# Slabs of the modulation weights as the stationary operand, three output tiles started together, one more buffer for split weights

## What is computed

```python
def ada_modulation(cvec, w, b):
    m = jax.nn.silu(cvec) @ w + b          # w: 1024 x 3072 per layer, cvec: c and c_ctx
    return jnp.split(m, 3, axis=-1)
hx = modulate(rmsnorm(x, norm_w[l]), shift_x[:, None], scale_x[:, None])   # h*(1+scale)+shift
px = split_proj(hx @ w_in[l])
...
mod = (c_act @ ada_w[i] + ada_b[i])[:, None, :]                            # second block, 6 x 1024 each
h = rmsnorm_2(x, norm_g[i, 0]) * (1.0 + sc_m) + sh_m
```

## Time and profile before

| | us |
|---|---|
| median of 3 runs (range) | 2013.99 (2012.77 to 2014.24) |
| profiled execution | 2014.52 |
| its span | 2012.7 |
| PE busy / PEld busy | 1940.7 / 1670.6 |
| DVE busy / ACT busy | 1420.9 / 903.8 |
| mean DMA rate | 149 GB/s |

### The profile page before, as it was taken

One profiled execution on the slowest core, in us unless ns is written; L12 is line 12 of the kernel. 1 busy time (PEld: TensorE's weight loads), 2 busy tenths in 40 slices (PEclk: granted clock), 3 DMA queues, 4 the chain that ended last, 5 costly groups with the idle time before them and its releaser, 6 DMA issues. The chain is left out here.

```text
span 2012.7 us, 31617 instructions
## 1 busy us (share of the span) xinstructions
PE 1940.7 (96%) x12194; PEld 1670.6 (83%) x12194; DVE 1420.9 (71%) x2648; ACT 903.8 (45%) x1657; POOL 0.2 (0%) x4
## 2 busy tenths in 40 slices
PE   7999999999999999999989999999999999999997
PEld 2788887767888887898878999687799979989997
DVE  1549956568889993677667997563688558968864
ACT  2422324545323332434456544464565546456553
POOL 0000000000000000000000000000000000000000
PEclk9999999999999999899999999999999999999999
DMA  8323321114666662543224986556555525135542
GB/s 271 124 87 101 90 78 42 42 32 157 199 205 202 201 199 84 163 152 105 84 74 137 290 281 225 174 162 199 193 184 184 165 92 168 64 105 189 184 163 95
DMA packets 293252, 299.21 MB, mean 149 GB/s; under 512 B 4960, under 2 KB 292704, under 8 KB 292976
## 3 DMA queue, kind: packets, MB, share of 16 engines
q1 hardware_dynamic: 293104, 297.19, 46.1%
HBM read 296.12 MB, written 1.05 MB: 148 GB/s over the span
## 5 line engine op out<-in xcount | busy, mean ns | idle before, releaser
L485 PE MATMUL bank<-h_hi,w_hi 128*128 128x256 f32 (+1 forms) x2912 | 929.8, 319 | 26.3 <-ACT h_hi L1094 7.2
L486 PE MATMUL bank<-h_lo,w_hi 128*128 128x256 f32 (+1 forms) x2912 | 915.1, 314 | 0.0
L487 PE MATMUL bank<-h_hi,w_lo 128*128 128x256 f32 (+1 forms) x2912 | 914.9, 314 | 0.0
L1525 DVE TENSOR_TENSOR w_lo<-ring,w_hi 128x1024 fp32r<-128x1024 f32 (+2 forms) x444 | 502.1, 1135 | 296.1 <-ACT w_hi L1008 282.2
L485 PEld LDWEIGHTS bank<-h_hi,w_hi 128*128 128x128 f32 x2912 | 557.4, 191 | 79.8 <-issue 14.6
L487 PEld LDWEIGHTS bank<-h_hi,w_lo 128*128 128x128 f32 x2912 | 557.7, 192 | 32.8
L486 PEld LDWEIGHTS bank<-h_lo,w_hi 128*128 128x128 f32 x2912 | 558.1, 192 | 32.1 <-issue 0.5
L1008 ACT ACTIVATE w_hi<-ring 128x1024 fp32r<-128x1024 f32 (+2 forms) x444 | 436.3, 986 | 186.1 <-PE bank L487 178.5
L994 ACT ACTIVATE work<-bank 128x512 f32<-128x512 f32 (+1 forms) x154 | 75.2, 503 | 338.1 <-PE bank L487 296.0
L994 ACT ACTIVATE arena<-bank 128x256 f32<-128x256 f32 (+5 forms) x152 | 65.6, 436 | 296.3 <-PE bank L487 168.9
L1604 DVE SCALAR_TENSOR_TENSOR stat<-arena,small,stat 128x256 f32<-128x256 f32 x398 | 161.5, 482 | 0.0
(11 more groups left out here) (205 smaller groups left out, 1649.3 us busy)
## 6 DMA issues: line engine op xcount, KB each, us to landing
ring<-in_w_in SPq DMA_DIRECT2D x86, 1024.0 KB, 5.4
ring<-in_ffn_w_up SPq DMA_DIRECT2D x44, 1024.0 KB, 5.1
arena<-in_ada_w SPq DMA_DIRECT2D x29, 1024.0 KB, 6.3
ring<-in_ada_w SPq DMA_DIRECT2D x19, 1024.0 KB, 5.2
ring<-in_w_branch SPq DMA_DIRECT2D x32, 512.0 KB, 5.0
arena<-in_w_mod SPq DMA_DIRECT2D x16, 1024.0 KB, 5.2
ring<-in_ffn_w_down SPq DMA_DIRECT2D x16, 1024.0 KB, 5.0
ring<-in_gla_w_in SPq DMA_DIRECT2D x12, 1024.0 KB, 5.3
```

The source lines that it names most:

```text
L485: pe.matmul(out, ws[0][:, k, :], hi, start=start, stop=False)
L486: pe.matmul(out, ws[0][:, k, :], lo, start=False, stop=False)
L487: return pe.matmul(out, ws[1][:, k, :], hi, start=False, stop=stop)
L1525: step(nc.vector.tensor_tensor(w_lo[u % PARTS][:, 0:nk, :], src, w_hi[u % PARTS][:, 0:nk, :].bitcast(F32), ALU.subtract), f"lo {u}", *(["u ...
```

## The change

- `mod_direct` replaces `mod_step`: the slab is the stationary operand (two halves of 128 columns, 8 k each), and one or two columns of the vector are streamed; the result comes out as columns, 16 matmuls for a slab. The row copies (`mod_row`) and the turns (L545) go; ACT only adds the bias (`mod_cols`); for slabs that come with a norm it does so from k = 4 of that norm on.
- `project_group` starts three tiles together (GROUP = 3): for each k it waits for the two parts of h once and does nine matmuls. It is used behind all norms but that of GLA, and at the start of both mixer output projections.
- PARTS goes from 3 to 4, AHEAD from 2 to 3, and `first_units` splits four units instead of two, on both engines. The scratch area for DMA descriptors is set smaller to make room.
- At the start SP loads a small part of the tables, x and the context first, then two slabs of `w_in`, then the eight modulation slabs into their own place in `arena`, in pairs of scale and shift. PE sums the squares first, does four modulation slabs, and the other four inside the first group at k = 2 and k = 4. The norm goes pair by pair on DVE.
- `keep_clock` counts: start 13 to 0; "n2 0" 6 to 9; ahead of the recurrent block's output 8 to 15; "n3 0" 6 to 9; "n3 1" 8 and 8 to 9 and 11; "n2 1" 8 and 10 to 9 and 12; ahead of GLA's output 7 to 12.
- The order of a few slabs in the stream changes, so that the two slabs of the first four units come ahead of modulation slabs.

```diff
-PARTS = 3
-AHEAD = 2
+PARTS = 4
+AHEAD = 3
+GROUP = 3
...
+START = [(4 + i, i) for i in range(4)]
...
+            def project_group(names, n, ready, hi=part(h_hi, 0), lo=part(h_lo, 0), before=None):
+                ws = [unit(name) for name in names]
+                outs = [open_bank(name) for name in names]
+                for k in range(KT):
+                    if before:
+                        before(k)
+                    ready(k)
+                    for name, w, out in zip(names, ws, outs):
+                        m = three_products(out[:, 0:n], w, k, hi(k, n), lo(k, n), k == 0, k == KT - 1)
...
-                    for k in range(KT):
-                        m = pe.matmul(out[0:vecs.shape[2], 0:256], vecs[:, k, :], w[:, k, :],
-                                      start=k == 0, stop=k == KT - 1)
...
+                for j in range(2):
                     for k in range(KT):
+                        ins = pe.matmul(out[:, nv * j:nv * j + nv], w[:, k, P * j:P * j + P], vecs[:, k, :],
+                                        start=k == 0, stop=k == KT - 1)
...
                 if l == 0:
-                    modulations("start", sum_squares("n1 0", 2 * S, KT))
-                    keep_clock(13)
+                    pe.wait_ge(early_landed, 16)
+                    sum_all("n1 0", 2 * S, KT)
+                    start_modulations(0)
+                    start_modulations(1)
...
             def first_units(tile):
-                split_to(unit_of[tile] + 1)
+                split_to(unit_of[tile] + PARTS - 1)
...
+                if pairs:
+                    for k in range(0, KT, 2):
+                        pairs(k)
+                        tile(k)
+                        tile(k + 1)
+                        low(k)
+                        low(k + 1)
+                    return
```

More of the change, by code:

```diff
@@ L299, in split_until @@
             return u
[L303 to L304 removed]
+        mod_at = {"n1 1": [("ada", 1, i) for i in range(5, 8)],
                   "fin": [("ada", 1, i) for i in range(8, 11)],
@@ L394, in program, with start_slot @@
         ffn_slabs(1)
[L396 to L403, removed]
+        def start_slot(i):
+            return carve(SLAB * i, KT, 256)
         def pair_before(l, b, i):
@@ L548, in modulations, with mod_direct @@
[L548 to L559, removed]
+            def mod_direct(m, w, free):
+                kind, l, i = m
+                vecs = csil[:, :, 0:2] if kind == "mod" else csil[:, :, 2:3]
+                nv = vecs.shape[2]
+                out = open_bank(f"sum {kind} {l}.{i}")
+                for j in range(2):
+                    for k in range(KT):
+                        ins = pe.matmul(out[:, nv * j:nv * j + nv], w[:, k, P * j:P * j + P], vecs[:, k, :],
+                                        start=k == 0, stop=k == KT - 1)
+                ins.then_inc(*tensor.does(f"filled sum {kind} {l}.{i}", *free))
@@ L791, in ffn @@
                 else:
[L792 to L797, removed]
+                    keep_clock(11)
+                todo = [f"{nm} {l}.{2 * i + j}" for i in range(11) for nm in ("ffg", "ffv") for j in range(2)]
+                project_group(todo[:GROUP], S, both_parts(f"n3 {l}"))
+                for name in todo[GROUP:]:
+                    project(name, S)
                 tag = f"ffn {l}"
@@ L1042, in deviation @@
                 evacuate(name, stat[:, 0:n], ACT.Sqrt, [f"dev {name}"], scale=1.0 / count, bias=eps)
[L1044 to L1064, removed]
             def mod_cols(m):
@@ L1079, in mod_cols, with modulated @@
                 a.then_inc(*scalar.does("emptied " + name, f"col {kind} {l}.{i}"))
[L1081 to L1088, removed]
+            def modulated(name, groups, shift, before=None):
                 for k in range(KT):
-                    if k < more:
-                        mod_row(at, k)
+                    if before:
+                        before(k)
                     act.wait_ge(*vector.did(f"normed {name}.{k}"))
@@ L1096, in modulated, with cols_at, before, start_cols @@
                     a.then_inc(*scalar.does(f"hi {name}.{k}"))
-                assert more <= KT
+            def cols_at(at):
+                def before(k):
+                    if k >= 4 and k - 4 < len(mod_at[at]):
+                        mod_cols(mod_at[at][k - 4])
+                return before
+            def start_cols(k):
+                if k % 2 == 0:
+                    for i in START[k // 2]:
+                        mod_cols(("mod", 0, i))
             act.wait_ge(params_landed, 16)
@@ L1304, in _ @@
             deviation("fin", S, D)
-            mod_rows("fin")
+            for m in mod_at["fin"]:
+                mod_cols(m)
             def pre_norm(name, ready, l, q, first, at=None):
@@ L1489, in normed @@
                 for k in range(KT + 2):
                     if k < KT:
-                        if k >= 4:
-                            after(f"lo {name}.{k - 4}")
-                        for g in groups:
-                            sl = slice(S * g, S * g + S)
-                            ins = nc.vector.scalar_tensor_tensor(dve_t[k % 4][:, sl], xT[:, k, sl], gain(k, g),
-                                                                 stat2[:, sl], ALU.mult, ALU.mult)
-                            step(ins, *([f"normed {name}.{k}"] if g == groups[-1] else []))
@@ L1498, in normed @@
-                    if k >= 2:
-                        i = k - 2
-                        dve.wait_ge(*scalar.did(f"hi {name}.{i}"))
-                        after(f"normed {name}.{i}")
-                        for g in groups:
-                            sl = slice(S * g, S * g + S)
-                            ins = nc.vector.scalar_tensor_tensor(h_lo[:, i, sl], dve_t[i % 4][:, sl], shift(i, g),
-                                                                 h_hi[:, i, sl].bitcast(F32), ALU.add, ALU.subtract)
-                            step(ins, *([f"lo {name}.{i}"] if g == groups[-1] else []))
+                        tile(k)
```

183 lines of the change are left out of this document (102 added, 81 removed).

## The result

| | before | after |
|---|---|---|
| median of 4 runs each, us | 2013.38 | 2058.64 (2053.14 to 2061.06) |
| ratio, 95% interval | 1 | 1.0221 (1.0199 to 1.0243) |
| span of the profiled execution, us | 2012.7 | 2055.9 |
| mean granted clock of TensorE | 0.993 | 0.958 |
| PE busy, us | 1940.7 | 2000.7 |

The changed kernel is 45 us slower. The forecast was 1985, range 1974 to 2018. Rival B of the prediction, to which it gave 0.20, came in with its time (about 2059) and with its mechanism, though not with its split of that time.

The account below looks back on a forecast made before the run. PE, busy 1940.7 of 2012.7 us, was taken as the bound, with its idle and slow stretches at the norms. The terms summed to -28.7, so 2014.52 became 1985.8 and, less 0.5, a median of 1985 us, range 1974 to 2018.

Parts of the forecast that it names:

- Rival B: Direct slabs lose the clock: about 19 of 27 run at 1.2 GHz, about 2059 us, 2030 to 2075; chance 0.20.
- the price of a direct slab: All modulation slabs: 3.5 us each against 3.80 for an old step; range 3.3 to 7.0, the latter at half clock.
- the point of decision: Number of cold direct slabs from which the clock loss decides against the gain: 28.7/3.5 = 8.
- The sum without the clock: Whole kernel: all terms add to -28.7 us, giving a median of 1985 us.
- start: Start: with the new load order and direct slabs the third projection ends at 65.5 instead of 80.94 us, -15.4.
- "n1 1": At this norm: with the group only nine products stay behind the last part of h, -8.5 us.
- "fin", "n2 0": At these norms: distance to third projection's end 10.6 to 8.6 us, two more units, faster slabs; -1.5 us.
- "rg" to "n3 0": First place: 6.6 us of keep_clock cover ACT, +0.5; second: distance 12.1 to 8.6, slabs, two units, -3.0 us.
- "n2 1": At this norm: two more units on DVE add 2.4 us, a unit wait of 1.54 goes; +0.9 us.
- GLA: GLA stage: a unit wait of 1.45 us goes, but the chain ahead carries four units; +1.2 us.
- "n3 1": At this norm: two more units add 2.4 us, distance 10.9 to 8.6 gives -2.3; +0.1 us.
- units elsewhere: Other stages: four buffers shrink the remaining unit waits; -3 us, from -4.4 to +4.

Follow-up runs that it names:

- e1: The changed kernel with each direct slab matmul streaming its vector repeated to 64 columns under the same weight load: 1987.33 us, ratio 0.9874.
- e2: The changed kernel with the vector of each direct slab matmul repeated to 16 columns: 2056.37 us, ratio 1.0219.
- e3: The kernel before with only the 19 slabs outside the start made direct, one column streamed: 2055.83 us, ratio 1.0218.
- e4: The kernel before with only the 19 slabs outside the start made direct, vector repeated to 64 columns: 2009.58 us, ratio 0.9984.
- e11: The changed kernel with the vector of each direct slab matmul repeated to 32 columns: 2052.35 us, ratio 1.0201.
- e7: e1 with the keep_clock counts of the kernel before outside the start: 1992.24 us, ratio 0.9898.
- e8: e1 with three first units instead of four ahead of the two MLPs and the two attention stages: 1987.06 us, ratio 0.9878.
- e9: e1 with the group of three tiles taken back only at the recurrent mixer's input: 1985.06 us, ratio 0.9869.
- e10: e9 with three first units at the MLPs, two at GLA's mixer and four elsewhere: 1978.60 us, ratio 0.9836.
- e5: e1 with the group of three tiles taken back everywhere (GROUP = 1): 1994.00 us, ratio 0.9910.
- e6: The kernel before with only four unit buffers, three ahead, four first units and the slab order this needs: 2022.17 us, ratio 1.0048.

## Why the prediction was wrong

**The step that failed is the weighing of rival B against the forecast**, and under it the price of a direct slab: 3.5 us, at full clock, for all 27. The changed kernel takes 149.8 us for the 27 slabs, 5.5 each on average and 6.8 where the clock is low. The prediction had both ends of that price (3.3 and 7.0), the place, the point of decision (8 cold slabs of 27) and a sum (2059, measured 2058.6). It took the low end on two rows that held 1.00: one with PE busy for 7.47 of 11.8 us, and one that it read as 18 us of old slabs. By the earlier trace rows the slabs start at 1260.75 there, so they fill 10 of the 18. Both stream 512 or 256 columns with every load. They bear on idle time and on thin stationary operands, not on a thin moving operand. The only row of the right kind, L523 in the earlier trace rows, was 1.25 us long, too short to show a clock of its own. The row that told the price of the step could not tell its clock. e1 to e4 and e11 show the mechanism; that B got 0.20 and the range left it out followed from reading nearness by how busy PE was.

Of the clock, the Trainium skill ("TensorE: Matmul & The Clock Gate", Part 1) says that the chip judges how busy PE has been. In the window from 25 to 45 us PE is busy for 20.00 of 20.00 us by the records and the clock is 0.50, so busy time as the profile counts it is not what decides here, and the measurement is to be followed.

**B's own sum** was right in part by luck. It had 66 us for 19 cold slabs and 7.5 for the products behind them. Against e1 the direct steps take 149.8 us instead of 95.8, so 54 more, as much as 16 or 17 cold slabs, and 18 more lie in the sums, the `keep_clock` and the projections around them. By place the clock costs 25.6 us at the start, 7.9 at "n1 1", 15.1 at "fin" and "n2 0" and 24.7 from "rg" to "n3 0"; 1.2 come back after that. The prediction gave B no price by place.

**The sum without the clock** is tested by e1: 1985 against 1987.3. Its terms:

| term | predicted | e1 by trace |
|---|---|---|
| start | -15.4 | -15.6 |
| "n1 1" | -8.5 | -8.2 |
| "fin", "n2 0" | -1.5 | -1.9 |
| "rg" to "n3 0" | -2.5 | +1.4 |
| "n2 1" | +0.9 | +1.2 |
| GLA | +1.2 | +1.3 |
| "n3 1" | +0.1 | +0.9 |
| units elsewhere | -3 | -7.3 |

Right by size does not mean right by reason. The start is the clearest case. By its own terms (11 and 9.2 to the end of the sums, 14 for the slabs, then 30.4) the prediction had 64.6 and not 65.5. In e1 it was 65.4, and in the four other kernels with the same start (e7 to e10) 66.1 to 67.3. The prices stood: a sum of squares, a slab (3.55 against 3.5), four units on DVE (4.63 against 4.7). But:

- The 8.5 us of "n1 1" were all to come from the group. By e5 the group is worth 5.6 there; 2.6 are left without it.
- The 2.0 and 3.5 us that "n2 0" and "n3 0" were to get from the groups came without them, as e5 shows, and by e4 and e6 from ACT's order. The prediction gave that order no price.
- The group at "n2 0" costs 3.7 us later (e5, e9). The prediction asked what a group does for its own three tiles, and not who waits for them.
- At "rg" I let 6.6 us of `keep_clock` cover ACT to the end. In e1 the projection starts 7.6 us after the first of these matmuls:

```profile
1341.42 6.69 PE L457 MATMUL bank<-tables 128*128 128x256 f32 x30
1349.02 0.36 PE L479 MATMUL bank<-h_hi,w_hi 128*128 128x256 f32 x1 [0.90 <-ACT h_hi L1320]
```

  PE waits for ACT behind them for as long as before (0.92, rows 7), so this costs 1.0 more than I had. With the group's 2.6 to 3.7 that closes the gap of 3.9 between -2.5 and +1.4. e7 shows that the count can't simply be cut.
- The extra buffer helps more than I gave (waits of PE 7.4 to 4.7, and 7 us in the stages without a norm, of which e6, without direct steps and groups, shows 6.6 between "n1 1" and "fin"), and four first units cost as the prediction's prices say (e6).

## What to carry to other kernels

Before a thin vector is streamed against large stationary operands, look for a row in which PE does just that for many microseconds, with its granted clock; a short one gives the pace but not the clock. If there is none, take the low clock as the likelier case, or stream the vector repeated and read the clock again: here 64 columns held it at no cost in pace, and 16 and 32 did not hold it. A group of tiles that fills PE behind a chain is worth it only where nobody waits for the first of them.

## What was not expected of the hardware

- A matmul of 128x128 fp32 weights takes 0.111 us an instruction with 64 columns streamed, by a stride of zero, 0.112 with two (changed kernel, 70.81 to 75, clock 1.00) and 0.104 with one in the earlier trace rows. With this one edit the mean granted clock goes from 0.958 to 0.997 and the kernel from 2058.6 to 1987.3 us.
- PE and its weight loads can be busy for all of 20 us (25 to 45 in the changed kernel) at a granted clock of 0.50.
- At that level the step slows down by nearly the whole ratio of the two clocks: 0.213 us against 0.112.
